# Projection of the second half as seven block products per unit, with a condition row in PSUM and hosted tiles moved between stages

## The reference

```python
def even_mixer(h_lat, h_ctx, w_in, conv_w, q_g, k_g, rpb, w_out, need_ctx):
    def query_side(p):
        gb, gc, u, q = jnp.split(p, [CONV_CH, 2 * CONV_CH, 3 * CONV_CH], -1)
        y_conv = gb * dwconv3(gc * u, conv_w)
        return y_conv, rms_norm_2(split_heads(q, NA_HEADS), q_g)
    def kv_side(p):
        k, v = jnp.split(p, 2, -1)
        return rms_norm_2(split_heads(k, NA_HEADS), k_g), split_heads(v, NA_HEADS)
    p_lat = h_lat @ w_in          # 1024 -> 3072: gate, c, u, q, k, v of 512 columns each
```

## Time and profile before

| | us |
| --- | --- |
| median of 3 runs | 3009.03 (3007.95 to 3010.87) |
| profiled execution, its own time | 3007.53 |
| its span in the trace | 3005.7 |
| PE busy | 2883.3 (96%) |
| DVE, ACT, POOL busy | 1462.9, 571.5, 614.7 |
| `EvenProject`, first to last product on PE | 176.83, from 1477.66 to 1654.49 |
| mean granted clock of PE | 0.985 of full |

### The profile page before, as it was taken

One profiled execution on the slowest core, in us unless ns is written; L12 is line 12 of the kernel. 1 busy time (PEld: TensorE's weight loads), 2 busy tenths in 40 slices (PEclk: granted clock), 3 DMA queues, 4 the chain that ended last, 5 costly groups with the idle time before them and its releaser, 6 DMA issues.

```text
span 3005.7 us, 36250 instructions
## 1 busy us (share of the span) xinstructions
PE 2883.3 (96%) x14576; PEld 2200.0 (73%) x14576; DVE 1462.9 (49%) x2715; ACT 571.5 (19%) x1144; POOL 614.7 (20%) x420
## 2 busy tenths in 40 slices
PE   7999999999999997999999999999999889999998
PEld 2347478888666666899644748888874568999998
DVE  2556376569676775326574437756542530000101
ACT  1215121100333343210220410000022511000000
POOL 0000045556100000388300006555500000000000
PEclk9999999999999999999999999999999989999999
DMA  7550045554232222444462024545331025877885
GB/s 273 182 187 31 33 164 189 175 189 153 61 85 73 54 71 84 155 169 153 144 216 83 29 71 182 189 147 169 118 111 54 1 84 177 286 273 269 280 295 172
DMA packets 287045, 438.08 MB, mean 146 GB/s; under 512 B 17081, under 2 KB 175480, under 8 KB 286874
## 3 DMA queue, kind: packets, MB, share of 16 engines
q1 hardware_dynamic: 250288, 329.77, 32.5%
q10 hardware_dynamic: 36586, 105.93, 10.2%
HBM read 434.61 MB, written 1.06 MB: 145 GB/s over the span
## 4 chain that ended last, share of the span: by engine, by line
PE 89%; DVE 5%; ACT 2%; issue 1%; POOL 1%; DVEq 0%; ACTq 0%; POOLq 0%
PE bank L1029 31%; PE bank L861 22%; PE bank L2734 11%; PE bank L2748 5%; PE bank L885 4%; PE bank L877 3%; PE bank L2317 1%; PE bank L2716 1%; PE bank L2310 1%; PE bank L2760 1%; PE bank L1908 1%; PE bank L1928 1%; PE bank L2302 1%; PE bank L1921 1%; PE bank L2301 0%
## 5 line engine op out<-in xcount | busy, mean ns | idle before, releaser
L1029 PE MATMUL bank<-arena,slot 128*128 128x256 f32 (+1 forms) x3704 | 677.1, 343 | 7.7 <-DVE arena L1009 2.9
L1029 PEld LDWEIGHTS bank<-arena,slot 128*128 128x128 f32 x3704 | 604.9, 191 | 72.3 <-issue 9.8
L1042 POOL TENSOR_TENSOR slot<-slot 128x512 f32<-128x512 f32 (+3 forms) x208 | 283.4, 1362 | 1577.2 <-DMA slot<-in_ffn_w 664.9
L861 PE MATMUL bank<-uT,slot 128*128 128x512 f32 (+2 forms) x1312 | 484.8, 525 | 0.0
L861 PEld LDWEIGHTS bank<-uT,slot 128*128 128x128 f32 (+1 forms) x1312 | 246.3, 190 | 213.4 <-issue 201.4
L1029 PE MATMUL bank<-uT,slot 128*128 128x256 f32 (+1 forms) x1728 | 334.3, 350 | 8.6 <-ACT uT L613 8.3
L1043 POOL TENSOR_TENSOR slot<-slot 128x512 f32<-128x512 f32 (+3 forms) x208 | 342.0, 1644 | 0.0
L1029 PEld LDWEIGHTS bank<-uT,slot 128*128 128x128 f32 x1728 | 290.1, 191 | 46.4 <-ACT uT L613 12.0
L2734 PEld LDWEIGHTS bank<-arena,slot 128*128 128x128 f32 x2816 | 315.2, 192 | 5.5 <-issue 5.5
L2734 PE MATMUL bank<-arena,slot 128*128 128x128 f32 x2816 | 316.2, 275 | 2.8 <-issue 2.7
L2819 DVE TENSOR_TENSOR arena<-bank,halves 128x256 f32<-128x256 f32 (+1 forms) x48 | 19.3, 403 | 431.8 <-ACT halves L2780 431.8
(11 more groups left out here) (373 smaller groups left out, 2822.2 us busy)
## 6 DMA issues: line engine op xcount, KB each, us to landing
slot<-in_ffn_w SPq DMA_DIRECT2D x42, 2048.0 KB, 8.8
slot<-in_moe_w SPq DMA_DIRECT2D x32, 2048.0 KB, 9.9
arena<-in_ada_wt ACTq DMA_DIRECT2D x100, 512.0 KB, 3.6
slot<-in_moe_w SPq DMA_DIRECT2D x32, 1408.0 KB, 8.8
rstd<-in_ada_wt ACTq DMA_DIRECT2D x48, 512.0 KB, 3.5
slot<-in_moe_w SPq DMA_DIRECT2D x16, 1536.0 KB, 9.1
slot<-in_ssd_w_in SPq DMA_DIRECT2D x32, 512.0 KB, 6.5
uT<-in_ada_wt ACTq DMA_DIRECT2D x28, 512.0 KB, 3.8
```

The source lines that it names most:

```text
L861: ins = pe.matmul(bank[0:m, 0:t1 - t0], w[:, k, c0:c0 + m], x[:, k, t0:t1], start=(k == 0), stop=(k == kt - 1))
L1029: ins = pe.matmul(bank[:, u * n:u * n + n], a[:, k, u * P:u * P + P], x[:, k, :], start=(k == 0), stop=(k == self.h - 1))
L1042: pool.tensor_tensor(out[:, :, 0:c], x[:, :, 0:c], y[:, :, 0:c], op)
```

## The change

1. `EvenProject` becomes `pooled` and makes its six blocks as six units of `Seven` (42 products of 8 matmuls of 256 columns). The sums are put between the products of k and gate, the flips between those of c. For v the roles are exchanged (`turned`): the tokens are the stationary operand and the 256 weight columns stream; `TokenTiles` places the blocks. The convolution of tiles 0 and 1 follows product S4 of unit u, that of tiles 2 and 3 product S3. Squares of heads 0 and 1 are made by ACT at the first `sum`, those of 4 and 5 at the fifth; each step of ACT's and DVE's list now ends with the loads and sums of its own place.
2. Hosted items: 16 instead of 24 in `EvenProject`; eight (one-sided) more in the first `HiddenRelu2`; the `Down` behind it hosts 8 one-sided and 24 two-sided items instead of 16 and 16.
3. For all guests but the first the latents' condition row is copied into `bank_pair` by ACT (at place 0, and where the block of weights changes), and the first sum of each item reads it there; the discarded output goes to SBUF.
4. Rooms, rows, sums of tokens and the raw bias get other places in the arena.

```diff
@@ AdaGuest
+                self.in_bank, self.copy_at = room is not early_guest, {}
+                if self.in_bank:
+                    blks = [blk for blk, _, _, _ in self.items]
+                    self.spare = self.rows[blks[0], 0]
+                    self.copy_at = {0: (0, 1)}
+                    if blks[0] != blks[-1]:
+                        n = blks.index(blks[-1])
+                        self.copy_at[places[n - 1] + self.items[n - 1][3] - 1] = (n, 2)
...
+            def row(self, blk, s):
+                return bank_pair[:, :, :] if self.in_bank and s == 0 else self.rows[blk, s]
...
             def loads(self, act, place):
+                if place in self.copy_at:
+                    n, _ = self.copy_at[place]
+                    act.wait_ge(rows_landed, 16 * (self.rows_before + len(self.needed())))
+                    act.wait_ge(guest_summed, self.first + n)
+                    act.activation(bank_pair[:, :, :], self.rows[self.items[n][0], 0], ACT.Copy).then_inc(rows_copied, 1)
@@ Seven.product
+                if turned:
+                    f = a.shape[2]
+                    for t in range(n // P):
+                        for k in range(self.h):
+                            ins = pe.matmul(bank[:, t * f:t * f + f], x[:, k, t * P:t * P + P], a[:, k, :], start=(k == 0),
+                                            stop=(k == self.h - 1))
@@ EvenProject
+            pooled = True
+                between = {(self.K, name): [("sum", j)] for j, name in enumerate(("22", "S2", "S4", "S3"))}
+                between.update({(self.GATE, name): [("sum", 4 + j)] for j, name in enumerate(("12", "S1", "22", "S2"))})
+                between.update({(self.C, name): [("flip", j)] for j, name in enumerate(Seven.ORDER[0:len(self.FLIPS)])})
+                order = []
+                for q, name in Seven.order(6):
+                    order += [(q, name)] + between.get((q, name), [])
...
@@ EvenProject.act
-                for n in range(2):
-                    head_square(act, self.head(n)[0], n, TOK)
                 for i, (kind, j) in enumerate(self.order):
-                    self.guest.loads(act, i - 1)
+                    if j == "11":
+                        Seven.act(act, B, self.units[kind], i)
                     if kind == "sum":
+                        if j in (0, 4):
+                            square(j)
+                            square(j + 1)
                         rstd_act(act, B, ch, j, i, TOK, 64, RMS_EPS)
+                        if j % 4 < 2:
+                            square(j + 2)
+                    self.guest.loads(act, i)
@@ EvenProject.dve
+                for step in (1, 2, 4, 3):
+                    self.seven.token_sum(dve, step)
...
+                        Seven.dve(dve, B, self.units[kind], self.at(kind), j)
+                        if kind == self.U and j in ("S4", "S3"):
+                            B.freed(dve, i)
+                            for tile in ((0, 1) if j == "S4" else (2, 3)):
+                                self.convolve(dve, ch, tile)
+                    self.guest.sums(dve, ch, i)
@@ stages
-        even_places = [3, 3] + [4] + [p + d for p in (6, 8, 10, 12, 14, 16, 18, 20, 23, 26) for d in (0, 1)] + [28]
+        even_places = spread(6, 30, 16)
-        hid = HiddenRelu2(I["ffn_w1"][0], TOK, AdaGuest(ada01[0:4], spread(5, 52, 32), hidden_guest))
+        hid = HiddenRelu2(I["ffn_w1"][0], TOK, AdaGuest(ada01[0:5], spread(5, 52, 40), hidden_guest))
-                             AdaGuest(ada01[4:6] + ada10[0:2], spread(4, 50, 32), down_guest))]
+                             AdaGuest(ada01[5:6] + ada10[0:3], spread(4, 50, 32), down_guest))]
-        stages += [EvenProject(AdaGuest(ada10[2:5], even_places, even_guest)), Attention(*even_attention(), 2),
+        stages += [EvenProject(AdaGuest(ada10[3:5], even_places, even_guest)), Attention(*even_attention(), 2),
```

More of the change, by code:

```diff
@@ L532, in __init__ @@
                 self.room, self.rows = room
-                self.spare = bank_pair[:, :, :]
-                if room is early_guest:
+                self.in_bank, self.copy_at = room is not early_guest, {}
[6 more added lines that the diff above has]
+                        self.copy_at[places[n - 1] + self.items[n - 1][3] - 1] = (n, 2)
+                    self.copies = {blk: i + 1 for i, blk in enumerate(sorted(set(blks)))}
+                    self.copies_before = sum(len(g.copy_at) for g in guests)
+                else:
                     self.spare = arena_at(22528, 2, 512)
@@ L988, in __init__ @@
                 room = room or h * n
+                places = at if isinstance(at, tuple) else [at + i * room for i in range(3)]
                 self.h, self.n = h, n
@@ L991, in __init__ @@
                 self.x21, self.x22 = x[:, h:kt, 0:n], x[:, h:kt, n:T]
-                self.t1, (self.t2, self.t3, self.t4) = self.x12, (arena_at(at + i * room, h, n) for i in range(3))
+                self.t1, (self.t2, self.t3, self.t4) = self.x12, (arena_at(c, h, n) for c in places)
                 self.right = {"11": self.x11, "12": self.x21, "S1": self.t1, "22": self.t4, "S2": self.t2, "S4": self.x22,
@@ L2186, in pe, with pool @@
                     else:
-                        feature_major(pe, B, i, w, j * P, uT, KD, 0, TOK)
-                    if kind in first and j == 3:
-                        W.used(full_sem, B.base + i + 1)
+                        q, name = kind, j
+                        streamed = None
+                        if name == "11":
+                            self.blocks.append(len(W.plan))
+                            views[q] = W.block(pe, [w_in[:, self.FIRST[q]:self.FIRST[q] + 512]], KD)
+                        if q == 0 and name in ("11", "12"):
+                            streamed = lambda: pe.wait_ge(*S("u_lat").taken("pe"))
+                        self.seven.product(pe, B.empty(pe, i), views[q], name, q == 0, streamed, turned=q == self.V)
+                        if name == "S3":
+                            W.used(full_sem, B.base + i + 1)
+                        if (q, name) == (0, "12"):
+                            S("u_ctx").passed("pe", KD)
+                            self.u_ready = S("u_lat").seen["pe"], S("u_ctx").seen["pe"]
+            def pool(self, pool, B, ch):
+                for q, n in enumerate(self.blocks):
+                    Seven.pool(pool, B, W.arrived(pool, n), self.at(q))
             def act(self, act, B, ch):
@@ L2211, in act @@
-                    if kind == "v" and j % 2:
-                        bank = B.full(act, i)
-                        act.activation(m_v[:, j, 0:512], bank[:, :], ACT.Copy).then_inc(*B.free(i))
+                        if j % 4 < 2:
+                            square(j + 2)
+                    self.guest.loads(act, i)
                 rstd_drop(act, 8)
             def dve(self, dve, B, ch):
-                dve_link(ch, dve.memset(arena[:, 15872:15872 + 8 * (LAT + 2)], 0.0))
+                pads = m_pad.rearrange("p j (s t) -> p (j s) t", t=LAT + 2)
@@ L2253, in dve @@
-                    if kind == "v" and j % 2 == 0:
-                        bank = B.full(dve, i)
-                        dve.tensor_copy(m_v[:, j, 0:512], bank[:, :]).then_inc(*B.free(i))
+                    else:
+                        Seven.dve(dve, B, self.units[kind], self.at(kind), j)
[3 more added lines that the diff above has]
+                                self.convolve(dve, ch, tile)
```

112 lines of the change are left out of this document (57 added, 55 removed).

## The result

| | before | after |
| --- | --- | --- |
| median, us | 3009.52 (3007.95 to 3010.87, 4 runs) | 3046.24 (3044.55 to 3049.11, 4 runs) |
| profiled execution | 3007.53 | 3044.55 |
| mean granted clock | 0.985 | 0.969 |

What follows compares the result with a forecast made beforehand. PE, busy 96% of the span, was taken to bound the kernel. Gains 15.6 + 1.45 - 0.75 = 16.3 us, given back 3.7 + 5.6 + 3.5 = 12.8, net 3.5: 3005.5 us, range 2997 to 3012.

Steps and rivals of the forecast that it cites:

- Work on PE, -19.7 us: `EvenProject`: 42 products at 3.455 us plus sums and flips take 157.2 us of PE instead of 176.8.
- start of the stage +4.1: Start of `EvenProject`: the first products wait for all latent tiles, ending at 1488.7 instead of 1484.6, 4.1 us given back.
- the two waits 3.7 and 5.6: First and fifth head sums in `EvenProject`: PE stands 3.7 and 5.6 us for ACT's squares, queued behind loads awaiting DVE.
- The clock behind the two waits, 3.5: Behind both head-sum waits PE's clock falls to half for about 3.5 us each, losing 1.75 each, 3.5 us together.
- No fall over a gap of 2.43 us: Read from the gap in `HiddenSwiglu`: over 2.43 us of idle PE the clock stayed at full.
- First sum from PSUM 1.30 us, no contention: DVE's first sum of a hosted item, row in PSUM: 1.30 us with handover, not the contested 1.9 or 2.3.
- ACT at the start: Start of `EvenProject`: ACT's row copy takes about 1.05 us, product 11's bank is free at 1506.7, 2.7 us to spare.
- Moved tiles at nothing: Hosted tiles moved to the first feed-forward and within `Down`: DVE's lag stays near 6 us, covered by banks, costing nothing.
- the wait for POOL in `HiddenSwiglu` gained: End of `HiddenSwiglu`: PE's 1.45 us wait for POOL goes away because hosted sums read PSUM, 1.45 us gained.
- The end, +0.75: Ahead of the attention: PE waits for DVE's addition of the last product, 1.45 us instead of 0.71, 0.75 more.
- rival 1: The two head-sum waits cost time but the clock stays up: 7.0 us gained, 3002.0 us; chance 0.20.

Runs made afterwards that it cites:

- e3_squares: Changed kernel with ACT's squares of heads 0, 1, 4 and 5 made one product earlier, ahead of the load ACT waits for: 3054.99 us, ratio 1.0135.
- e8_guests: Kernel before with only the condition row in PSUM and the moved hosted tiles, `EvenProject` keeping its old tiles: 3005.52 us, ratio 0.9985.
- e10_fill_fifth: Changed kernel with six 512-column matmuls in front of the fifth sum only, the gap ahead of the attention left: 3060.05 us, ratio 1.0171.
- e1_fill: Changed kernel with two unused 512-column matmuls behind the last product of `EvenProject`, ahead of the attention: 3012.47 us, ratio 1.0009.
- e5_fill1: Changed kernel with one unused 512-column matmul behind the last product of `EvenProject`, leaving a 0.55 us gap: 3013.57 us, ratio 1.0012.
- e11_later: Changed kernel with eight 512-column matmuls (about 7 us) in front of the first product of unit v: 3053.03 us, 3 of 4 executions slow.
- e13_later2: Changed kernel with two 512-column matmuls (1.7 us) in front of the first product of unit v: 3014.47 us, 0 of 10 executions slow.
- e14_later4: Changed kernel with four 512-column matmuls (3.5 us) in front of the first product of unit v: 3051.05 us, 3 of 4 executions slow.
- e7_before_gap2: Kernel before with two unused DVE additions behind the last copy of v, gap 2.66 us ahead of the attention: 3072.18 us, ratio 1.0207.

## Why the prediction was wrong

Point by point:

- **Work on PE, -19.7 us, start of the stage +4.1, the two waits 3.7 and 5.6**: right. The waits were 3.53 and 5.39, the gap at the start 2.44. The way they come about (ACT waits at a load for a second sum of DVE, the squares are queued behind it) was right too: `e3_squares` moves the squares ahead of the load, and the first wait is gone, the second 1.86.
- **The clock behind the two waits, 3.5**: a little short. The clock is at half for 3.4 us at the first wait and for 6.8 at the second. From the start of the sum to that of the next product it is 1.87 us instead of 0.86, and the products behind take 3.95 and 5.41 instead of 3.45: 1.5 and 3.0 us, 4.5 in all. The stage came to 175.4 instead of "about 174".
- **No fall over a gap of 2.43 us**: read from one record, and not a rule. All 17 traces have this gap at the start of `HiddenSwiglu`, and in 12 of them the clock falls there for 3.4 us (that of `e8_guests` is shown above; before and after are among the other five). At the start of `EvenProject`, where the prediction counted the gap but no clock, 8 of the 12 traces with the seven products have such a fall, 1.7 us each; the profiled execution of the kernel after has none.
- **First sum from PSUM 1.30 us, no contention**: right. Of the records with the row in PSUM none is over 1.22 us, though in 32 of the 75 below POOL was at work for more than half of the time; the sums with both inputs in SBUF still reach 2.32:

```profile
L602 DVE SCALAR_TENSOR_TENSOR arena<-arena x87: 1210/1222/2316, 64.1 to 1970.7; 128x1024 f32<-128x1024 f32 x87
...
L602 DVE SCALAR_TENSOR_TENSOR arena<-arena,bank_pair x75: 1205/1215/1222, 408.3 to 2083.0; 128x1024 f32<-128x1024 f32 x75
```

- **ACT at the start**: the row's copy takes 1.03 and stands at 1504.53; the copy of product 11 follows at 1505.50 and costs PE nothing, as predicted.
- **Moved tiles at nothing, the wait for POOL in `HiddenSwiglu` gained**: right in its direction. The distance between the two traces shrinks there from 33.6 to 31.9 us, and `Down` has no gap.
- **The end, +0.75**: here is the step that failed. The wait itself was right (1.40 forecast as 1.45). The step priced it as what PE stands still and gave no thought to the clock. The clock had a part of its own, but only for the two long waits, and of the 2.43 us gap in front of dense products it said that the clock stayed up; so a gap of 1.4 us seemed safe. What stands behind the gap wasn't asked. Behind the gaps at the sums come dense products, and the clock is back after 3.4 and 6.8 us. Behind this one comes the attention with matmuls of 64 to 256 columns: there the clock stayed at half for 75 us (109 in `e3_squares` and in `e10_fill_fifth`), 34 us lost. With the gap filled and nothing else changed the kernel takes 3012.5 us (`e1_fill`), 0.5 above the upper end of the range given: the fall of the clock is 34 of the 41 us by which the forecast was off.

No rival had this either: rival 1 spoke of clock and phase, and only as something that could spare time.

The trace of before held a warning. In its windows at the router, where matmuls of 8 to 128 columns run:

```profile
2444.00:2467.00 23.00, 15.01 (x67) 14.22 (x68) 15.08 (x69) 2.99 (x6) 0.00 (x0) 0.50 0.27 92
2468.00:2480.00 12.00, 12.00 (x29) 5.32 (x28) 2.08 (x3) 2.39 (x4) 0.00 (x0) 1.00 0.01 1
```

The clock is at half for 23 us and back when matmuls of 512 columns begin. As a warning it is weaker than the attention, for PE also stood still there for 8 of the 23 us. The rows that the prediction read for the clock were three gaps in front of other work.

The Trainium skill ("TensorE: Matmul & The Clock Gate", on the HAM clock gate) says that the chip's watch on PE runs freely of the kernel, so that the same kernel shows the change of clock at another matmul from run to run. The kernels of which only some executions fall bear this out (2 of 10, 3 of 10, 3 of 4 and 3 of 4); in others the outcome is the same each time (4 of 4, 0 of 10), so that the moment is not free there, and no run shows what ties it. The page also lists the full clock for a PE that has been busy for a short while; here the rows disagree, with PE busy for 40.00 of 40.00 us at 0.50.

**What is shown and what isn't.** Shown: the loss is the clock in the attention; it needs the gap (`e5_fill1`, and none of 44 executions high with the gap filled); a gap of 2.66 us brought it 5 times of 5, one of 1.4 us by its moment (`e11_later`, `e13_later2`, `e14_later4`, and the table). Argued only, from the table: that the waits inside the stage act through that moment, by stepping the clock and shifting what follows. Open: what ends the half clock in the attention, which in the kernel after comes back at 1730.0 in the middle of the stage, among the same small matmuls; why the kernel before with the 1.4 us gap falls in 2 and 3 of 10 executions at both positions; where the few executions of the other kind in `e11_later` and `e14_later4` come from (their traces weren't taken); and why without a fall in the attention the kernel after is no faster than before, where `e8_guests` alone is 4.7 us faster. The last is in part counted: the trace of `e13_later2` shows falls at 1489, 1527 and 1554 of 3.4, 3.4 and 6.8 us, half of which is lost as far as PE works in them, some 6 us together, and that of `e8_guests` has none in that stage.

## What to carry to other kernels

A wait on the bottleneck engine has two prices: the idle time, and the clock of what stands behind it. In front of dense work the second is a few microseconds; in front of a long run of small matmuls it can be far more (34 to 60 us here, on a stage of 74), so such a handover has to be short (up to 0.72 us did no harm here), or be covered with matmuls that compute nothing: two of them, 1.9 us, gave back 34. And since a short gap does harm or not by its moment, a change somewhere else that shifts it can turn a fast kernel into a slow one: look at the granted clock in every stage behind the edit, and judge an edit with that gap filled, or one measures where the gap has landed instead of the edit.

## What the runs showed of the hardware that wasn't expected

- In the attention, with its matmuls of 64 to 256 columns, the half clock holds for 75 to 109 us of PE that is busy without a break (137 in `e7_before_gap2`, where it ends at 1791.4, 4 us into the output projection with its 512 columns). Behind the gaps ahead of dense products of 256 or 512 columns it lasted 3.4 or 6.8 us.
- In the attention the clock doesn't fall in the gap but 1.1 to 2.0 us after PE has resumed (1.9 in the kernel after, 1.6 in `e3_squares`, 1.4 in `e10_fill_fifth`, 1.1 in `e7_before_gap2`).
- The same gap, ahead of the same work, brings a fall in one execution or kernel and not in another: 12 of 17 traces at the gap of 2.43 us in `HiddenSwiglu`.
- With the condition row in PSUM, DVE's sum isn't slowed by POOL in any of the 75 records shown (at most 1.22 us); with both inputs in SBUF it took up to 2.32.
